# Making the low part of every fourth gate and up chunk by an adding transfer instead of VectorE

## The chip, the cores and the metric

The kernel runs on one core of one Trainium2 chip. The metric is the device time of one execution in microseconds (us). Three runs of the kernel before took 1509.71 to 1509.88 us, median 1509.78 us.

## The reference, cut to what matters

A decoder layer on 256 tokens of width 2048: a normalised projection, two kinds of attention, gates and an output projection, then the part that the change touches, a feed-forward network, and after it a gated embedding and a last norm. All in float32:

```
h = rmsnorm(x, g_ffn)                                    # 256 x 2048
x = x + (silu(h @ w_ffn_gate) * (h @ w_ffn_up)) @ w_ffn_down   # D_FF = 5632
```

w_ffn_gate and w_ffn_up are 2048 x 5632, w_ffn_down is 5632 x 2048.

## The kernel before, in words

Each product is made in three passes of a reduced float32 type (fp32r): a number is split into a high part (rounded to fp32r) and a low part (the number minus its high part), and TensorE adds high x high, low x high and high x low.

**Chunks and units.** Weights stream from HBM in chunks of 512 KB, 128 partitions x 1024 float32. In the feed-forward network a chunk is two row tiles of 512 columns each (KW = 2, WIDE = 512). Four chunks make a unit, and there are four slots (SLOTS), so chunk j of every unit lives in slot j of three buffers: ws (as loaded), hs (high part), ls (low part). One block of 512 feed-forward columns (`ff_pair`) takes four units: two of the gate, two of the up weights. There are 11 blocks (N_FFN), so 44 units and 176 chunks.

**Who does what to a chunk.** SP loads it (L259, `load`) once the low part of the same slot's chunk in the unit before has been made (`slot_free`, semaphore l_split). ScalarE makes the high part (L382, `split_high`) once the chunk has landed and TensorE has finished with the same slot of the unit before (semaphore chunk_used). VectorE makes the low part (L663, `split_low`: ws minus hs) once the high part is there (h_split). TensorE (`by_token`) waits for the high part, does eight matmuls with hs (L1192), waits for the low part (l_split) and does four with ls (L1197); the last counts up chunk_used.

**What lies between the chunks.** After the fourth chunk of a block's first unit TensorE makes eight transposes (L1282, `ff_columns`) of the last block's result, which ScalarE copies (L602, `ff_hi`) and VectorE subtracts (L1014, `ff_low`). After the second unit ScalarE makes the silu (L592), after the fourth VectorE multiplies (L1007).

**Order.** Each engine's instructions stand in a fixed, hand-written order and each engine works through them in that order. GpSimd (POOL) has nothing to do from the end of the attention on. No DMA of the kernel before is issued by GpSimd; SP issues the weights, and ScalarE four small or single transfers.

Of the kernel before, what the change touches and what calls it, by code (L numbers as in the profile page):

```python
# [6 lines left out]
ALU = mybir.AluOpType  # L7
ACT = mybir.ActivationFunctionType
# [17 lines left out]
KW = 2  # L26
# [43 lines left out]
C_PLE = C_DOWN + FF_CH * N_WIDE  # L70
C_END = C_PLE + PLE_CH * N_WIDE
HOOK = 3


D_VB = 1 + 4 + 4 + 4
# [33 lines left out]
def hybrid_layer(nc, c_rows, x, p, positions, g_mix, w_in, b_f, w_o_a, w_o_b, w_out, g_ffn, w_ffn_gate,  # L109
# [125 lines left out]
    sq_sum, rms_sqrt, rms_ready = S("sq_sum"), S("rms_sqrt"), S("rms_ready")  # L235
    p_t, p_high, p_ready = S("p_t"), S("p_high"), S("p_ready")
    ff_silu, ff_s, ff_t, ff_high, ff_ready = map(S, ("ff_silu", "ff_s", "ff_t", "ff_high", "ff_ready"))
    last_used, ple_sig, ple_out, y_scaled = S("last_used"), S("ple_sig"), S("ple_out"), S("y_scaled")
    y_ready_0, y_ready_1 = S("y_ready_0"), S("y_ready_1")

# [3 lines left out]
    @block.sync  # L244
    def _(sp):

        for b in range(2):
            sp.dma_start(x_tok[:, b, :], x_rows[:, b, :]).then_inc(x_loaded[b], 16)
        for n, g in enumerate((g_mix[0], g_ffn[0], g_ple[0])):
            sp.dma_start(gain_rows[n * KT:(n + 1) * KT, :], g.rearrange("(t q) -> t q", q=P)).then_inc(gains_loaded, 16)  # L250
        sp.dma_start(bias_f[F_ROWS, :], b_f[0].rearrange("(h o) -> h o", o=1)).then_inc(bias_loaded, 16)

        def slot_free(u, j):

            sp.wait_ge(l_split, 4 * (u - 1) + j + 1)

        def load(j, src, n=CHUNK):
            parts = src.shape[1]
            sp.dma_start(ws[:, j, 0:n].rearrange("p (t n) -> p t n", t=parts), src).then_inc(w_loaded[j], 16)  # L259


        sp.wait_ge(ring_zero, SLOTS)
        for j in range(SLOTS):
            slot = ws[:, j, 0:SMALL].rearrange("p (t n) -> p t n", t=KC)
            rows = win_t[:, KC * j:KC * j + KC, :]
            for at, col, n in ((0, AT_KI, D_IDX + H_IDX), (F_ROW, AT_FB, HB)):
                sp.dma_start(slot[:, :, at:at + n], rows[:, :, col:col + n]).then_inc(w_loaded[j], 16)

        def columns(u0, units, w, col0):

            with sp.Fori(0, units) as i:
                for j in range(SLOTS):
                    slot_free(u0 + i, j)
                    load(j, w[:, KC * j:KC * j + KC, ds(col0 + i * GROUP, GROUP)])

        columns(U_QI, 4, win_t, AT_QI)
        columns(U_QB, 8, win_t, AT_QB)

        def wide_columns(u0, units, w, col0):

            with sp.Fori(0, units) as i:
                for c in range(K_CH):
                    slot_free(u0 + c // SLOTS + i * (K_CH // SLOTS), c % SLOTS)
                    load(c % SLOTS, w[:, KW * c:KW * (c + 1), ds(col0 + i * WIDE, WIDE)])

        wide_columns(U_VB, 2, win_t, AT_VB)
        wide_columns(U_GA, N_WIDE, win_t, AT_GA)
        columns(U_QA, 6, win_t, AT_QA)
        wide_columns(U_GB, N_WIDE, win_t, AT_GB)
        with sp.Fori(0, N_WIDE) as i:  # L290
            for c in range(K_CH):
                slot_free(U_WO + c // SLOTS + i * 2, c % SLOTS)
                w, t = (wob_t, woa_t)[c // SLOTS], KW * (c % SLOTS)
                load(c % SLOTS, w[:, t:t + KW, ds(i * WIDE, WIDE)])

        sp.wait_ge(o_ready, FREE + HEADS)
        sp.dma_start(p_tok[:, :, :], p_rows).then_inc(p_loaded, 16)
        wide_columns(U_OUT, N_WIDE, wout_t, 0)
        with sp.Fori(0, N_FFN) as i:
            for half, w in enumerate((wgate_t, wup_t)):  # L300
                for c in range(K_CH):
                    slot_free(U_FFN + 2 * half + c // SLOTS + i * 4, c % SLOTS)
                    load(c % SLOTS, w[:, KW * c:KW * (c + 1), ds(i * WIDE, WIDE)])
        for n in range(N_WIDE):
            for c in range(FF_CH):
                at = C_DOWN + FF_CH * n + c
                slot_free(at // SLOTS, at % SLOTS)
                load(at % SLOTS, wdown_t[:, KW * c:KW * (c + 1), WIDE * n:WIDE * (n + 1)])
        for n in range(N_WIDE):
            cols = slice(WIDE * n, WIDE * (n + 1))  # L310
            for c in range(PLE_CH):
                at = C_PLE + PLE_CH * n + c
                slot_free(at // SLOTS, at % SLOTS)
                load(at % SLOTS, wpp_t[:, :, cols] if c == 0 else wpg_t[:, KW * (c - 1):KW * c, cols])

        for n in range(4):
            cols = slice(D_MODEL // 4 * n, D_MODEL // 4 * (n + 1))
            for b in range(2):
                sp.wait_ge((y_ready_0, y_ready_1)[b], n + 1)
                sp.dma_start(out_rows[:, b, cols], out_tok[:, b, cols]).then_inc(out_stored, 16)  # L320
        sp.wait_ge(out_stored, 8 * 16)

    @block.gpsimd
    def _(pool):
# [42 lines left out]
        with pool.Fori(0, HA) as h:  # L367
            stage_head(HB + h, h, h // (HA // HA_KV), D_VA + 1)


    @block.scalar
    def _(act):
# [161 lines left out]
        for n in range(N_WIDE):  # L534
# [5 lines left out]
                act.activation(gates[:, gate, :, cols], gates[:, gate, :, cols], ACT.Sigmoid).then_inc(gate_ready, 1)  # L540
            split_chunks(C_WO + 8 * n + 8, 4)

        def squares(stage, n):

            act.wait_ge(x_new, 4 * stage + n + 1)
# [18 lines left out]
        for n in range(N_WIDE):  # L564
# [5 lines left out]
            else:  # L570
                squares(0, n - 1)
                new_high(0, n - 1, (n - 1) % 2)
            split_chunks(C_OUT + 8 * n + 8, 4)

        def ff_pair(i, step, first=False):

            u = U_FFN + 4 * step + i * 8
            c = step + i * 2
            for j in range(SLOTS):
                split_high(u + 1, j)  # L580
            if first:
                squares(0, 3)
                new_high(0, 3, 1)
                root(0)
            else:
                ff_hi(c - 1, (step + 1) % 2)
            for j in range(SLOTS):
                split_high(u + 2, j)
            if first:
                act.wait_ge(rms_ready, 1)  # L590
            for b in range(2):
# [1 line left out]
            ins.then_inc(ff_silu, 1)  # L593
            for j in range(SLOTS):
                split_high(u + 3, j)
            for j in range(SLOTS):
                split_high(u + 4, j)

        def ff_hi(c, pair):

# [1 line left out]
            act.activation(ff[:, ds(c * 4, 4), 0:TOK], four(side[:, 2 * pair:2 * pair + 2, :]), ACT.Copy).then_inc(ff_high, 1)  # L602

        ff_pair(0, 0, first=True)
        with act.Fori(0, (N_FFN - 1) // 2) as i:
            ff_pair(i, 1)
            ff_pair(i, 2)

        for n in range(N_WIDE):
            at = C_DOWN + FF_CH * n  # L610
# [46 lines left out]
    def _(dve):  # L657
# [314 lines left out]
        for n in range(N_WIDE):  # L972
# [5 lines left out]
                                  ALU.subtract).then_inc(p_ready, 1)  # L978
            else:
                new_low(0, n - 1, (n - 1) % 2)  # L980
            split_chunks(C_OUT + 8 * n + 8, 4)
            dve.wait_ge(chunk_used, C_OUT + 8 * n + 8)
            new_x(n, (n + 1) % 2)

        def ff_pair(i, step, first=False):

            u = U_FFN + 4 * step + i * 8
            c = step + i * 2
            for j in range(SLOTS):
                split_low(u + 1, j)  # L990
            if first:
                new_low(0, 3, 1)
# [2 lines left out]
                dve.wait_ge(rms_ready, 1)  # L995
            else:
                ff_low(c - 1, (step + 1) % 2)
            for j in range(SLOTS):
                split_low(u + 2, j)
            for j in range(SLOTS):  # L1000
                split_low(u + 3, j)
            for j in range(SLOTS):
                split_low(u + 4, j)
            dve.wait_ge(ff_silu, c + 1)
            dve.wait_ge(chunk_used, 4 * (u + 4))
# [9 lines left out]
                              ff[:, ds(c * 4, 4), 0:TOK].bitcast(F32), ALU.subtract).then_inc(ff_ready, 1)  # L1015

        ff_pair(0, 0, first=True)
        with dve.Fori(0, (N_FFN - 1) // 2) as i:
            ff_pair(i, 1)
            ff_pair(i, 2)  # L1020

        for n in range(N_WIDE):
            at = C_DOWN + FF_CH * n
# [51 lines left out]
    def _(pe):  # L1075
# [108 lines left out]
                unit(U_QB + n, U_QB + n, hn, (U_QB + e) % 2)  # L1184
                dots(n)

        def by_token(at, slot, tiles, src, banks, first, last, width=WIDE, halves=False):

            def high_part(b):
                for q, k in enumerate(tiles):  # L1190
# [8 lines left out]
                return mm  # L1199

            pe.wait_ge(h_split, at + 1)
            if halves:
                pe.wait_ge(l_split, at + 1)
                for b in range(2):
                    high_part(b)
                    low_part(b).then_inc(last_used, 1)
            else:
                for b in range(2):
                    high_part(b)
                pe.wait_ge(l_split, at + 1)  # L1210
                for b in range(2):
                    mm = low_part(b)
                mm.then_inc(chunk_used, 1)
# [122 lines left out]
        def ff_pair(i, step, first=False, reused=True):  # L1336
# [5 lines left out]
            else:  # L1342
                pe.wait_ge(ff_silu, pair_n)
            for half in range(2):
                if half == 1 and first:
                    pe.wait_ge(x_new, 4)
                elif half == 1:
                    pe.wait_ge(ff_s, pair_n)
                for c in range(K_CH):
                    if first and half == 0:  # L1350
                        pe.wait_ge(xg_ready, KW * (c + 1))
                    by_token(at + K_CH * half + c, c % SLOTS, range(KW * c, KW * (c + 1)), xg, pair_of(acc, 1 - half), c == 0, c == K_CH - 1)
# [15 lines left out]
        for n in range(N_WIDE):  # L1368
            pe.wait_ge((ff_silu, ff_s, x_new, x_new)[n], (N_FFN, N_FFN, 5, 6)[n])
            for c in range(FF_CH):  # L1370
                if n == 0:
                    pe.wait_ge(ff_ready, (KW * c + 1) // 4 + 1)
                at = C_DOWN + FF_CH * n + c
                by_token(at, at % SLOTS, range(KW * c, KW * (c + 1)), ff, pair_of(acc, (n + 1) % 2), c == 0, c == FF_CH - 1)
# [7 lines left out]
        for n in range(N_WIDE):  # L1382
# [6 lines left out]
            for c in range(PLE_CH):  # L1389
                at = C_PLE + PLE_CH * n + c  # L1390
                if c == 0:
                    by_token(at, at % SLOTS, range(KT_PLE), p_cols, pair_of(side, pair), True, True)
                else:
                    if n == 0:
                        pe.wait_ge(xg_ready, KT + KW * c)
                    by_token(at, at % SLOTS, range(KW * (c - 1), KW * c), xg, pair_of(acc, pair), c == 1, c == K_CH,
                             halves=at == C_END - 1)
                if c == HOOK and n == 0:
                    new_columns(1, 3, 0)

# [41 lines left out]
```

## Time and profile before

| | |
|---|---|
| median of three runs | 1509.78 us |
| the profiled execution's own time | 1509.83 us |
| its span, first to last instruction | 1508.0 us |
| granted TensorE clock, mean | 0.997 |
| TensorE matmuls busy | 1480.2 us, 98% |
| VectorE busy | 855.5 us, 57% |
| ScalarE busy | 692.7 us, 46% |
| GpSimd busy | 50.0 us, 3% |
| moved by DMA | 278.87 MB, mean 185 GB/s |

"Busy" counts the time in which an engine has an instruction running. "PE" is TensorE's matmul side, "PEld" its weight loading, which overlaps it; DVE is VectorE, ACT is ScalarE, POOL is GpSimd, SPq is SP's instruction queue. A group of instructions names its line, its output and input tiles, its shape, how many there are, their busy time and the mean of one, and then how long the engine sat idle just before them and what released it.

### The profile page before, as it was taken

The page shows a single profiled execution, that of the slowest core. Times are in us where ns is not written, and L with a number is a line of the kernel's source. Part 1 is how long each engine was busy: PE and PEld are TensorE (multiplying, and loading weights), DVE is VectorE, ACT ScalarE, POOL GpSimd, SP SyncE. Part 2 cuts the span into 40 slices and gives each one's busy share as a digit, 9 for nine tenths or more (in the row PEclk, how much of TensorE's full clock was granted, in tenths as well). Part 3 has the DMA queues.
Part 4 walks back from the last instruction along what each step waited for, and adds up shares of the span by engine and source line. Part 5 has one row for each costly group of instructions (what it writes and reads, how often), then busy time and mean ns, then how long its engine had stood idle before and what let it go on. Part 6 is the DMA issues. An engine that isn't in the chain of part 4 may idle for free.

```text
span 1508.0 us, 19540 instructions
## 1 busy us (share of the span) xinstructions
PE 1480.2 (98%) x7025; PEld 1241.6 (82%) x7025; DVE 855.5 (57%) x987; ACT 692.7 (46%) x847; POOL 50.0 (3%) x80
## 2 busy tenths in 40 slices
PE   5999999999999999999999999999999999999996
PEld 5888888888888888888888888888888888888885
DVE  6966776657655565555445454444545444454654
ACT  5644444544444544545444444444444343443544
POOL 0021001100210000000000000000000000000000
PEclk9999999999999999999999999999999999999998
DMA  6665565566555665566666666566666666666663
GB/s 191 185 194 177 173 194 178 163 185 197 171 168 168 185 199 181 182 193 186 192 184 194 185 192 194 183 192 184 193 184 193 193 185 194 191 186 195 196 212 109
DMA packets 165486, 278.87 MB, mean 185 GB/s; under 512 B 12920, under 2 KB 50224, under 8 KB 164912
## 3 DMA queue, kind: packets, MB, share of 16 engines
q1 hardware_dynamic: 164832, 275.77, 59.6%
q10 hardware_dynamic: 592, 2.24, 0.4%
q8 instruction: 43, 0.70, 0.2%
q14 instruction: 19, 0.16, 0.0%
HBM read 275.87 MB, written 2.11 MB: 184 GB/s over the span
## 4 chain that ended last, share of the span: by engine, by line
PE 96%; DVE 2%; DMA 1%; ACT 0%; issue 0%; ACTq 0%; DVEq 0%
PE acc L1192 51%; PE acc L1197 26%; PE acc L1088 8%; PE acc L1097 4%; PE side L1192 2%; PE side L1197 1%; PE side L1282 1%; DMA rope_c<-in_rope_rows 1%; DVE ls L663 1%; PE side L1227 0%; DVE hn L718 0%; PE side L1233 0%; PE side L1241 0%; PE side L1242 0%; PE side L1240 0%
## 5 line engine op out<-in xcount | busy, mean ns | idle before, releaser
L663 DVE TENSOR_TENSOR ls<-ws,hs 128x1024 fp32r<-128x1024 f32 (+1 forms) x520 | 633.9, 1226 | 585.0 <-ACT hs L382 581.7
L382 ACT ACTIVATE hs<-ws 128x1024 fp32r<-128x1024 f32 (+1 forms) x520 | 548.0, 1057 | 737.8 <-PE acc L1197 611.0
L1192 PE MATMUL acc<-hs,xg 128*128 128x512 f32 x1664 | 412.4, 390 | 0.0
L1192 PEld LDWEIGHTS acc<-hs,xg 128*128 128x128 f32 x1664 | 311.5, 188 | 64.1
L1197 PE MATMUL acc<-ls,xg 128*128 128x512 f32 x832 | 222.6, 389 | 0.0
L1197 PEld LDWEIGHTS acc<-ls,xg 128*128 128x128 f32 x832 | 156.2, 188 | 32.6
L1192 PE MATMUL acc<-hs,ff 128*128 128x512 f32 x704 | 174.3, 390 | 0.0
L1192 PE MATMUL acc<-hs,hn 128*128 128x512 f32 (+1 forms) x704 | 171.9, 387 | 0.0
L1192 PEld LDWEIGHTS acc<-hs,ff 128*128 128x128 f32 x704 | 131.9, 188 | 27.2
L1192 PEld LDWEIGHTS acc<-hs,hn 128*128 128x128 f32 x704 | 127.1, 188 | 24.2
L1088 PE MATMUL acc<-hn,hs 128*128 128x512 f32 x560 | 139.2, 392 | 0.0
L1088 PEld LDWEIGHTS acc<-hn,hs 128*128 128x128 f32 x560 | 101.5, 189 | 18.9
L1197 PE MATMUL acc<-ls,ff 128*128 128x512 f32 x352 | 94.1, 389 | 0.0
L1197 PE MATMUL acc<-ls,hn 128*128 128x512 f32 (+1 forms) x352 | 90.4, 380 | 0.0
L1097 PEld LDWEIGHTS acc<-hn,ls 128*128 128x128 f32 x560 | 74.2, 191 | 4.7 <-DVE ls L663 0.3
L1197 PEld LDWEIGHTS acc<-ls,ff 128*128 128x128 f32 x352 | 66.1, 188 | 13.7
L1097 PE MATMUL acc<-hn,ls 128*128 128x256 f32 x560 | 75.9, 283 | 0.0
L1197 PEld LDWEIGHTS acc<-ls,hn 128*128 128x128 f32 x352 | 64.2, 188 | 13.1
L1192 PE MATMUL acc<-hs,mixed 128*128 128x512 f32 x256 | 63.6, 391 | 0.0
L1192 PEld LDWEIGHTS acc<-hs,mixed 128*128 128x128 f32 x256 | 47.8, 188 | 9.7
L499 ACT ACTIVATE lg<-lg,neg_max 128x128 f32<-128x128 f32 (+1 forms) x32 | 14.3, 448 | 47.0 <-DVE neg_max L878 47.0
L1197 PE MATMUL acc<-ls,mixed 128*128 128x512 f32 x128 | 34.2, 389 | 0.0
(188 smaller groups left out, 812.0 us busy)
## 6 DMA issues: line engine op xcount, KB each, us to landing
ws<-in_w_in SPq DMA_DIRECT2D x152, 512.0 KB, 3.9
ws<-in_w_ffn_gate SPq DMA_DIRECT2D x88, 512.0 KB, 3.5
ws<-in_w_ffn_up SPq DMA_DIRECT2D x88, 512.0 KB, 3.5
ws<-in_w_ffn_down SPq DMA_DIRECT2D x88, 512.0 KB, 3.6
ws<-in_w_out SPq DMA_DIRECT2D x32, 512.0 KB, 3.7
ws<-in_w_ple_gate SPq DMA_DIRECT2D x32, 512.0 KB, 4.3
ws<-in_w_o_b SPq DMA_DIRECT2D x16, 512.0 KB, 4.1
ws<-in_w_o_a SPq DMA_DIRECT2D x16, 512.0 KB, 3.8
```

The costliest lines, as they stand in the source:

```text
L382: act.activation(hs[:, j, 0:n], ws[:, j, 0:n], ACT.Copy).then_inc(h_split, 1)
L499: act.activation(lg[:, cols], lg[:, cols], ACT.Exp, bias=neg_max[:, b:b + 1], accum_out=sums[:, b:b + 1]).then_inc(exp_done, 1)
L663: dve.tensor_tensor(ls[:, j, 0:n], ws[:, j, 0:n], hs[:, j, 0:n].bitcast(F32), ALU.subtract).then_inc(l_split, 1)
L1088: mm = pe.matmul(acc_of(bank + m, 2 * TOK), hs[:, j, at], src[:, k, :], start=first and q == 0, stop=last and q == len(tiles) - 1)
L1097: mm = pe.matmul(acc_of(bank + m, TOK), ls[:, j, at], src[:, k, 0:TOK], start=False, stop=False)
L1192: pe.matmul(banks[b], src[:, k, part * TOK + b * P:part * TOK + (b + 1) * P], hs[:, slot, q * width:(q + 1) * width], start=first and q == ...
L1197: mm = pe.matmul(banks[b], src[:, k, b * P:(b + 1) * P], ls[:, slot, q * width:(q + 1) * width], start=False, stop=last and q == len(tiles ...
L1282: mm = pe.transpose(bank[m // 2][:, m % 2 * TOK + b * P:m % 2 * TOK + (b + 1) * P], rows[:, b, at + m * P:at + (m + 1) * P], ident[:, :])
```

## The change

In the 44 gate and up units the low part of slot 3 (ADDED) is no longer made by VectorE. ScalarE, right after the high part, writes the negated high part into ls (a copy of ws with scale -1, rounded to fp32r), and GpSimd then issues a transfer that reads the same 512 KB of weights from HBM a second time and adds them onto ls in SBUF. TensorE waits for that transfer's semaphore before the low matmuls of this chunk. SP reloads slot 3 of ws once the negated part has been made. The counts of l_split after these units are lower by 44 (N_ADD). The loops of SP, ScalarE and VectorE are partly unrolled for the first and last steps.

```
+ADDED = SLOTS - 1
+U_ADD = U_FFN
+N_ADD = 4 * N_FFN
+def lows(u, j):
+    return 4 * U_ADD + ADDED * (u - U_ADD) + j + 1
...
+        def slot_taken(u, j):                                  # SP, before a load
+            if j == ADDED:
+                sp.wait_ge(neg_high, u - U_ADD)
+            else:
+                sp.wait_ge(l_split, lows(u - 1, j))
...
+        def add_weights(n, w, rows, cols):                     # GpSimd
+            pool.wait_ge(neg_high, n + 1)
+            pool.dma_start(ls[:, ADDED, :].rearrange("p (t n) -> p t n", t=KW), w[:, rows, cols],
+                           accum_op=ALU.add).then_inc(low_added, 16)
+        for i in range(N_FFN):
+            for half, w in enumerate((wgate_t, wup_t)):
+                for q in range(2):
+                    k = KW * (SLOTS * q + ADDED)
+                    add_weights(2 * half + q + i * 4, w, slice(k, k + KW), slice(i * WIDE, i * WIDE + WIDE))
...
+        def negative_high():                                   # ScalarE
+            act.activation(ls[:, ADDED, :], ws[:, ADDED, :], ACT.Copy, scale=-1.0).then_inc(neg_high, 1)
...
             for j in range(SLOTS):                             # ScalarE, ff_pair
                 split_high(u + 1, j)
+            negative_high()
             if first:
                 squares(0, 3)
...
             for j in range(SLOTS):
                 split_high(u + 2, j)
+            negative_high()
             if first:
                 act.wait_ge(rms_ready, 1)
...
-            for j in range(SLOTS):                             # VectorE, ff_pair, four times
+            for j in range(ADDED):
                 split_low(u + 1, j)
...
             pe.wait_ge(h_split, at + 1)                        # TensorE, by_token
+            low = (l_split, at + 1) if low is None else low
...
                 for b in range(2):
                     high_part(b)
-                pe.wait_ge(l_split, at + 1)
+                pe.wait_ge(*low)
...
+                             low=(low_added, 16 * (u + c // SLOTS - U_ADD) + 16) if c % SLOTS == ADDED
+                             else (l_split, lows(u + c // SLOTS, c % SLOTS)))
```

## Rows read from the trace of the kernel before

**Rows 1.** The page: busy us, share and instructions of each engine; then the chain's shares
```profile
PE 1480.2 (98%) x7025; PEld 1241.6 (82%) x7025; DVE 855.5 (57%) x987; ACT 692.7 (46%) x847; POOL 50.0 (3%) x80
...
PE 96%; DVE 2%; DMA 1%; ACT 0%; issue 0%; ACTq 0%; DVEq 0%
```

**Rows 2.** Busy time by stretch, one inside gate and up; last: PEclk, DMA share, GB/s
```profile
0.00:100.00 100.00, 84.74 (x480) 74.42 (x481) 78.88 (x121) 55.83 (x82) 9.07 (x22) 1.00 0.66 193
...
700.00:1100.00 400.00, 400.00 (x1802) 331.93 (x1801) 199.12 (x172) 171.67 (x171) 0.00 (x0) 1.00 0.62 189
```

**Rows 3.** Waits, 655 to 1135 us: who for whom, us in total, times, longest
```profile
ACT hs L382 <- PE acc L1197: 267.6, 169, 1.7
DVE ls L663 <- ACT hs L382: 237.6, 170, 2.3
```

**Rows 4.** Groups by form, whole span
```profile
L663 DVE TENSOR_TENSOR ls<-ws,hs 128x1024 fp32r<-128x1024 f32 x516 | 631.2, 1230 | 585.0 <-ACT hs L382 581.7 <-DVE sel L824 1.4 <-DVE q_idx L785 0.3
L382 ACT ACTIVATE hs<-ws 128x1024 fp32r<-128x1024 f32 x516 | 545.3, 1060 | 737.8 <-PE acc L1197 611.0 <-PE acc L1097 63.8 <-PE acc L1088 25.1
L1197 PE MATMUL acc<-ls,xg 128*128 128x512 f32 x832 | 222.6, 389 | 0.0
...
L1197 PE MATMUL acc<-ls,hn 128*128 128x512 f32 x320 | 85.9, 390 | 0.0
```

**Rows 5.** Timeline inside one block: start us, length us, engine, line, tiles
```profile
887.46 1.06 ACT L382 ACTIVATE hs<-ws 128x1024 fp32r<-128x1024 f32 x1 [1.66 <-PE acc L1197]
890.18 1.06 ACT L382 ACTIVATE hs<-ws 128x1024 fp32r<-128x1024 f32 x1 [1.66 <-PE acc L1197]
...
897.01 0.87 PEld L1197 LDWEIGHTS acc<-ls,xg 128*128 128x128 f32 x4
...
898.35 1.06 ACT L382 ACTIVATE hs<-ws 128x1024 fp32r<-128x1024 f32 x1 [1.67 <-PE acc L1197]
...
899.33 1.03 ACT L602 ACTIVATE ff<-side 128x1024 f32 x1
```

**Rows 6.** Timeline, later in the same block
```profile
908.82 0.87 PEld L1197 LDWEIGHTS acc<-ls,xg 128*128 128x128 f32 x4
...
911.11 1.25 ACT L592 ACTIVATE silu_g<-acc,rms 128x512 f32<-128x512 f32 x2
```

**Rows 7.** Transfers: kind of issue, count, KB each, median us from issue to landing
```profile
ws<-in_w_ffn_gate SPq DMA_DIRECT2D x88, 512.0 KB, 3.5
...
x_tok<-in_x SPq DMA_DIRECT2D x2, 1024.0 KB, 7.7
...
c_keys<-c_rows ACTq DMA_DIRECT2D x1, 1024.0 KB, 6.2
g_out<-in_g_final ACTq DMA_DIRECT2D x1, 1024.0 KB, 8.0
```

**Rows 8.** The tile ws, 700 to 1100 us: landing of its loads
```profile
DMA to landing us min/median/max: 3.3/3.5/4.6
```

**Rows 9.** Timeline at the c_keys transfer, which runs beside weight loads
```profile
181.89 0.36 ACTq L484 DMA_DIRECT2D c_keys<-c_rows  x1
...
185.36 1.06 ACT L382 ACTIVATE hs<-ws 128x1024 fp32r<-128x1024 f32 x1 [2.48 <-DMA ws<-in_w_in]
...
189.22 1.06 ACT L382 ACTIVATE hs<-ws 128x1024 fp32r<-128x1024 f32 x1 [2.80 <-DMA ws<-in_w_in]
```

**Rows 10.** Timeline at the g_out transfer
```profile
1407.60 12.18 SPq L259 DMA_DIRECT2D ws<-in_w_ple_gate  x5
...
1408.81 0.35 ACTq L629 DMA_DIRECT2D g_out<-in_g_final  x1
```

**Rows 11.** GpSimd's nearest instructions, groups by form
```profile
L354 POOL COPY q_st<-q_cols 128x256 f32 x16 | 18.0, 1126 | 87.1 <-DVE k_cols L902 73.8 <-DVE k_cols L671 12.4
...
L350 POOL TENSOR_TENSOR qi_l<-q_idx,qi_h 128x256 fp32r<-128x256 f32 x8 | 12.8, 1596 | 0.6
```

More of the change, by code:

```diff
@@ L237, in hybrid_layer @@
     ff_silu, ff_s, ff_t, ff_high, ff_ready = map(S, ("ff_silu", "ff_s", "ff_t", "ff_high", "ff_ready"))
+    neg_high, low_added = S("neg_high"), S("low_added")
     last_used, ple_sig, ple_out, y_scaled = S("last_used"), S("ple_sig"), S("ple_out"), S("y_scaled")
@@ L253, in slot_free @@
         def slot_free(u, j):
-            sp.wait_ge(l_split, 4 * (u - 1) + j + 1)
+            if isinstance(u, int) and u > U_ADD + N_ADD:
+                sp.wait_ge(l_split, 4 * (u - 1) + j + 1 - N_ADD)
+            else:
+                sp.wait_ge(l_split, 4 * (u - 1) + j + 1)
+        def slot_taken(u, j):
+            if j == ADDED:
+                sp.wait_ge(neg_high, u - U_ADD)
+            else:
+                sp.wait_ge(l_split, lows(u - 1, j))
         def load(j, src, n=CHUNK):
@@ L298, in _ @@
         wide_columns(U_OUT, N_WIDE, wout_t, 0)
-        with sp.Fori(0, N_FFN) as i:
+        for j in range(SLOTS):
+            slot_free(U_FFN, j)
+            load(j, wgate_t[:, KW * j:KW * (j + 1), 0:WIDE])
+        for half, w in enumerate((wgate_t, wup_t)):
+            for c in range(0 if half else SLOTS, K_CH):
+                slot_taken(U_FFN + 2 * half + c // SLOTS, c % SLOTS)
+                load(c % SLOTS, w[:, KW * c:KW * (c + 1), 0:WIDE])
+        with sp.Fori(1, N_FFN) as i:
             for half, w in enumerate((wgate_t, wup_t)):
                 for c in range(K_CH):
-                    slot_free(U_FFN + 2 * half + c // SLOTS + i * 4, c % SLOTS)
+                    slot_taken(U_FFN + 2 * half + c // SLOTS + i * 4, c % SLOTS)
                     load(c % SLOTS, w[:, KW * c:KW * (c + 1), ds(i * WIDE, WIDE)])
@@ L306, in _ @@
                 at = C_DOWN + FF_CH * n + c
-                slot_free(at // SLOTS, at % SLOTS)
+                if at < C_DOWN + SLOTS:
+                    slot_taken(at // SLOTS, at % SLOTS)
+                else:
+                    slot_free(at // SLOTS, at % SLOTS)
                 load(at % SLOTS, wdown_t[:, KW * c:KW * (c + 1), WIDE * n:WIDE * (n + 1)])
@@ L368, in _ @@
             stage_head(HB + h, h, h // (HA // HA_KV), D_VA + 1)
+        def add_weights(n, w, rows, cols):
[3 more added lines that the diff above has]
+        for i in range(N_FFN):
+            for half, w in enumerate((wgate_t, wup_t)):
+                for q in range(2):
+                    k = KW * (SLOTS * q + ADDED)
+                    add_weights(2 * half + q + i * 4, w, slice(k, k + KW), slice(i * WIDE, i * WIDE + WIDE))
     @block.scalar
@@ L573, in _, with ff_pair @@
             split_chunks(C_OUT + 8 * n + 8, 4)
-        def ff_pair(i, step, first=False):
+        negative_high()
+        def ff_pair(i, step, first=False, more=True):
             u = U_FFN + 4 * step + i * 8
@@ L588, in ff_pair @@
                 split_high(u + 2, j)
+            negative_high()
             if first:
@@ L595, in ff_pair @@
                 split_high(u + 3, j)
+            negative_high()
             for j in range(SLOTS):
                 split_high(u + 4, j)
+            if more:
+                negative_high()
         def ff_hi(c, pair):
@@ L604, in _ @@
         ff_pair(0, 0, first=True)
-        with act.Fori(0, (N_FFN - 1) // 2) as i:
+        with act.Fori(0, (N_FFN - 1) // 2 - 1) as i:
             ff_pair(i, 1)
             ff_pair(i, 2)
+        ff_pair((N_FFN - 1) // 2 - 1, 1)
+        ff_pair((N_FFN - 1) // 2 - 1, 2, more=False)
         for n in range(N_WIDE):
@@ L980, in _, with ff_pair @@
                 new_low(0, n - 1, (n - 1) % 2)
-            split_chunks(C_OUT + 8 * n + 8, 4)
+            split_chunks(C_OUT + 8 * n + 8, 4 if n < N_WIDE - 1 else ADDED)
             dve.wait_ge(chunk_used, C_OUT + 8 * n + 8)
             new_x(n, (n + 1) % 2)
-        def ff_pair(i, step, first=False):
+        def ff_pair(i, step, first=False, more=True):
             u = U_FFN + 4 * step + i * 8
             c = step + i * 2
-            for j in range(SLOTS):
+            for j in range(ADDED):
                 split_low(u + 1, j)
@@ L997, in ff_pair @@
                 ff_low(c - 1, (step + 1) % 2)
-            for j in range(SLOTS):
+            for j in range(ADDED):
                 split_low(u + 2, j)
-            for j in range(SLOTS):
+            for j in range(ADDED):
                 split_low(u + 3, j)
-            for j in range(SLOTS):
+            for j in range(ADDED if more else SLOTS):
                 split_low(u + 4, j)
@@ L1017, in _ @@
         ff_pair(0, 0, first=True)
-        with dve.Fori(0, (N_FFN - 1) // 2) as i:
+        with dve.Fori(0, (N_FFN - 1) // 2 - 1) as i:
             ff_pair(i, 1)
             ff_pair(i, 2)
+        ff_pair((N_FFN - 1) // 2 - 1, 1)
+        ff_pair((N_FFN - 1) // 2 - 1, 2, more=False)
         for n in range(N_WIDE):
@@ L1185, in _, with by_token @@
                 dots(n)
-        def by_token(at, slot, tiles, src, banks, first, last, width=WIDE, halves=False):
+        def by_token(at, slot, tiles, src, banks, first, last, width=WIDE, halves=False, low=None):
             def high_part(b):
@@ L1209, in by_token @@
                     high_part(b)
-                pe.wait_ge(l_split, at + 1)
+                pe.wait_ge(*low)
                 for b in range(2):
@@ L1344, in ff_pair @@
             for half in range(2):
+                u = U_FFN + 4 * step + 2 * half + i * 8
                 if half == 1 and first:
@@ L1351, in ff_pair @@
                         pe.wait_ge(xg_ready, KW * (c + 1))
-                    by_token(at + K_CH * half + c, c % SLOTS, range(KW * c, KW * (c + 1)), xg, pair_of(acc, 1 - half), c == 0, c == K_CH - 1)
+                    by_token(at + K_CH * half + c, c % SLOTS, range(KW * c, KW * (c + 1)), xg, pair_of(acc, 1 - half), c == 0, c == K_CH - 1,
+                             low=(low_added, 16 * (u + c // SLOTS - U_ADD) + 16) if c % SLOTS == ADDED
+                             else (l_split, lows(u + c // SLOTS, c % SLOTS)))
                     if c == HOOK and half == 0:
@@ L1373, in _ @@
                 at = C_DOWN + FF_CH * n + c
-                by_token(at, at % SLOTS, range(KW * c, KW * (c + 1)), ff, pair_of(acc, (n + 1) % 2), c == 0, c == FF_CH - 1)
+                by_token(at, at % SLOTS, range(KW * c, KW * (c + 1)), ff, pair_of(acc, (n + 1) % 2), c == 0, c == FF_CH - 1,
+                         low=(l_split, at + 1 - N_ADD))
                 if c == HOOK and n == 0:
@@ L1391, in _ @@
                 if c == 0:
-                    by_token(at, at % SLOTS, range(KT_PLE), p_cols, pair_of(side, pair), True, True)
+                    by_token(at, at % SLOTS, range(KT_PLE), p_cols, pair_of(side, pair), True, True, low=(l_split, at + 1 - N_ADD))
                 else:
@@ L1396, in _ @@
                     by_token(at, at % SLOTS, range(KW * (c - 1), KW * c), xg, pair_of(acc, pair), c == 1, c == K_CH,
-                             halves=at == C_END - 1)
+                             halves=at == C_END - 1, low=(l_split, at + 1 - N_ADD))
                 if c == HOOK and n == 0:
```

## The prediction

> **What bounds the kernel now.** I read the page first. TensorE's matmuls are busy for 98% of the span and hold 96% of the chain that ended last; VectorE, from which the change takes work, is busy for 57% and holds 2% of the chain [rows 1]. The next view is the table by stretches: inside the gate and up stage TensorE is busy for all 400 of 400 us, VectorE for 199, ScalarE for 172, GpSimd for none, and the DMA engines for 0.62 of the time [rows 2]. The list of waits says why the two helpers idle: ScalarE waited 267.6 us of that stage for TensorE to release slots, and VectorE 237.6 us for ScalarE's high parts; nobody on TensorE's side waited for either [rows 3]. So VectorE is not late, it is fed late, and nothing in this stage is gained by sparing it. The timeline gives the beat: ScalarE's high parts start at 887.46 and 890.18, so a chunk takes 2.72 us on TensorE, which is its twelve matmuls without a gap; from slot 3 of one unit (887.46) to slot 3 of the next (898.35) it is 10.89 us, four chunks [rows 5].
>
> **What is removed.** VectorE loses 44 of its low parts at 1.23 us each, 54 us [rows 4]. They lie under TensorE's matmuls and end nothing: credit 0. If VectorE's load slowed TensorE in some hidden way there would be a gain; the low matmuls are 389 and 390 ns in the stages with xg and with hn, although VectorE's load differs between them [rows 4], so I take 0 here too.
>
> **What is added to ScalarE.** 44 negated copies of the size of a high part, 1.06 us each [rows 4], 47 us in a stage where ScalarE is busy for 172 of 400 us [rows 2]. Back to back a second instruction starts 0.98 us after a high part (898.35 to 899.33), so the negated copy ends 0.98 + 1.06 = 2.04 us after the high part of slot 3 began, inside the 2.72 us until the next slot is released [rows 5]. What stands behind it moves by about 1 us: the copy L602, which nobody needs for blocks, and the silu of 1.25 us [rows 5, 6], whose output is needed at the next block, about eight chunks later. After the silu the next high part starts about 1 us late, with three chunks (8.16 us) until its use. Cost 0; the cover is that lead of three chunks.
>
> **What is moved in SP.** Slot 3 of ws is reloaded after the negated copy instead of after VectorE's low part: 2.04 us against 1.06 + 1.23 = 2.29 us after the high part starts [rows 4]. Nothing is behind it that this hurts: 0.
>
> **What is added to GpSimd and to the DMA engines, and the new wait.** This is the whole question. GpSimd has nothing else to do in this stage [rows 2], so each transfer is issued as soon as the negated copy ends, at 887.46 + 2.04 = 889.50. Before, TensorE began the low part of the same slot (its weight loading) at 897.01 [rows 5]. So the transfer has 7.51 us from issue to landing. In one unit of four the eight transposes stand in this stretch: 898.35 + 2.04 = 900.39 to 908.82, 8.43 us [rows 5, 6]. If it takes L, TensorE stops for L - 7.5 in 33 units and L - 8.4 in 11. Behind the waiting matmuls stands everything of TensorE, in order: the end of this chunk, with it the release of slot 3 to ScalarE, so the next negated copy and the next transfer start late by the same amount. A late transfer is thus paid in every unit and never caught up, while an early one costs nothing at all.
>
> How long is L? The trace before has no adding transfer and none issued by GpSimd. Lower end: a plain 512 KB load issued by SP beside its kind lands in 3.5 us, 4.6 at most [rows 7, 8]. But the adding transfer must read the weights and also the old content of ls, so it handles 1024 KB of input for 512 KB of output. The rows with 1024 KB took 6.2 us (c_keys), 7.7 (x_tok, two at a time at the start) and 8.0 us (g_out); the first and the last ran beside weight loads, as this one would [rows 7, 9, 10]. That such a transfer and the weight loads share the engines is seen at c_keys: ScalarE had to wait 2.48 and 2.80 us for its weights, which it otherwise does not [rows 9]. Upper end: 8.0 us, and the time in which GpSimd writes out the transfer. For that there is no row; its nearest instructions take 1.13 and 1.60 us [rows 11], so 9.6 us in all. I take the row that is nearest in size and company, 8.0, and half of GpSimd's 1.13 us, since a transfer can start before its last piece is written out: L = 8.6 us.
>
> The sum: 33 x (8.6 - 7.5) = 36 us, and 11 x (8.6 - 8.4) = 2 us, together 38 us. The profiled execution took 1509.83 us (span 1508.0 and 1.8 around it), 0.05 us over the median of the three runs, so one number serves: 1510 + 38 = 1548 us. The ends: L at 7.5 or less gives 1510; L = 9.6 gives 33 x 2.1 + 11 x 1.2 = 82 us, 1592. TensorE's clock stays out of the sum: in the first 100 us the matmuls were busy for only 84.74 and 1.00 was granted [rows 2], and a stop of 1.1 in 12 us is less than that.
>
> A rule speaks against this L. The Trainium skill, "DMA: Bandwidth & Descriptors", section "Anatomy of one DMA — SWDGE (gpsimd) path", puts a transfer at about 2.0 us plus its bytes over 436 GB/s; an estimate by it is 3.2 us for 512 KB and 4.4 us for twice the bytes, and the sum would be 0. For 512 KB the trace is near it (3.5), for 1024 KB it is not (6.2 to 8.0) [rows 7], and I go by the rows. For the doubling of the input the same skill has a page, "Collectives: The Full Stack", section "The bandwidth ceiling: the fold count and why AG ≠ RS ≠ AR": an add in the transfer needs two source reads for each piece and ran at about half the rate of a copy; no row of this trace has such an add.
>
> **Rivals.**
>
> (a) *The transfer is hidden anyway*, the other side of my forecast: it lands within 7.5 us, the low part of slot 3 is there before TensorE asks, and the time stays 1510 us, within 1 us. For it: the plain load's 3.5 us leaves 4 us for everything that is special here, c_keys at 6.2 us would still fit with 1.1 us to spare for GpSimd, and g_out and x_tok may be slow for reasons of their own (a row spread over all partitions; two at once at the start). The rule above is of this kind. Against it: the two larger rows. It decides at L = 7.5 us, a point 1.1 us from my value.
>
> (b) *The DMA engines become the bound.* They are busy for 0.62 of a unit's 10.89 us, 6.75 us, so 1.69 us for each of four loads [rows 2, 5]. An adding transfer that costs them twice a load makes 6.75 + 3.4 = 10.1 us, which just fits; from 2.45 loads on it does not. At four loads it is 13.5 us a unit, 2.6 over, and 44 x 2.6 = 115 us: 1625 us. For it: an add may handle its pieces one by one, read and then write. Against it: nothing in the trace shows one. Then weight loads would land late as well, and ScalarE would wait for ws, not only TensorE for the added part.
>
> (c) *Sparing VectorE gives something back*, through a memory port or otherwise, so that TensorE's 2.72 us a chunk shrinks. At 1% of the stage it would be 44 x 0.11 = 5 us: 1505 us. Against it: no matmul that waits, and the same mean at different VectorE loads [rows 3, 4].
>
> That a quarter of the low parts would not leave VectorE is excluded by the code; its count must fall by 44.
>
> **How the numbers follow.** Chances: my forecast (late by 0.1 to 2.4 us a unit) 0.46, hidden (a) 0.40, DMA engines bound (b) 0.11, gain (c) 0.03. The forecast's own range is 1513 to 1600: its upper end is a little past L = 9.6, where the starts of the next transfers crowd. Below 0.2% (3 us) I count as no change, about the least that a measurement of this kernel can tell apart. So faster 0.03, same 0.40, slower 0.46 + 0.11 = 0.57. The range is 1508 to 1600: it holds (a), all of the forecast, and leaves out (c) and most of (b), about 0.13.
>
> **What would show each step.** VectorE's ls group x472 instead of x516 and 54 us less; a new ScalarE group on ls from ws, x44 at 1.06 us, each beginning 0.98 us after a high part of slot 3. GpSimd's transfers with their time to landing: that median is L, and the table of transfers shows it directly; above 7.5 the matmuls of L1197 wait for it, 33 times longer by 0.9 than the other 11. Weight loads landing later than 3.5 us but ScalarE not waiting for ws. A DMA share near 0.85 in the stage instead of 0.62. The down stage unchanged. I am wrong if the median is under 7.5 us (then (a)), if ScalarE waits for ws again and again (then (b)), or if the beat of a chunk that waits for nothing differs from 2.72 us.

## The result and the profile after

The changed kernel takes 1535.45 us (median of four, 1535.25 to 1539.03) against 1509.76 us: ratio 1.0176, 95% interval 1.0163 to 1.0188, 25.7 us slower. The forecast was 1548 us. The profiled execution is the slowest of the four, 1539.03 us with a span of 1537.2, so its own difference to the one before is 29.2 us.

The page's busy line after, and the shares of the chain that ended last (before: [rows 1]):

```profile
PE 1489.0 (97%) x7025; PEld 1238.6 (81%) x7025; DVE 802.7 (52%) x943; ACT 732.8 (48%) x891; POOL 102.4 (7%) x124
...
PE 77%; DMA 15%; issue 3%; ACT 3%; DVE 2%; ACTq 0%; POOL 0%; DVEq 0%; POOLq 0%
```

TensorE has the same 7025 matmuls. What is new is the 15% of DMA and 3% of ScalarE in the chain, which was 96% TensorE. The groups, by form, of the lines that changed (VectorE's low parts: [rows 4]):

```profile
L713 DVE TENSOR_TENSOR ls<-ws,hs 128x1024 fp32r<-128x1024 f32 x472 | 577.1, 1230 | 603.1 <-ACT hs L421 600.0 <-DVE sel L874 1.4 <-DVE q_idx L835 0.3
...
L583 ACT ACTIVATE ls<-ws 128x1024 fp32r<-128x1024 f32 x44 | 45.9, 1042 | 0.0
...
L401 POOL DMA_DIRECT2D ls<-in_w_ffn_gate x22 | 26.4, 1198 | 417.1 <-ACT ls L583 417.1
L401 POOL DMA_DIRECT2D ls<-in_w_ffn_up x22 | 26.2, 1192 | 232.2 <-ACT ls L583 232.2
```

VectorE's low parts are 44 fewer and take 54.1 us less, and it idles 18 us longer for ScalarE instead. GpSimd's instruction for a transfer takes 1.19 us. The queues with their shares of the engines' span, and the transfers with the median from issue to landing ([rows 7]):

```profile
q1 hardware_dynamic: 164832, 275.77, 57.7%
q0 software_dynamic: 11968, 23.07, 9.4%
...
ws<-in_w_ffn_gate SPq DMA_DIRECT2D x88, 512.0 KB, 4.7
ws<-in_w_ffn_up SPq DMA_DIRECT2D x88, 512.0 KB, 4.6
...
ls<-in_w_ffn_gate POOLq DMA_DIRECT2D x22, 512.0 KB, 8.0
ls<-in_w_ffn_up POOLq DMA_DIRECT2D x22, 512.0 KB, 8.1
```

The adding transfers land after 8.0 us, counted from the start of GpSimd's instruction; the weight loads, 3.5 us before, take 4.7. The waits of the stage (655 to 1170 us) that belong to it:

```profile
POOL ls L401 <- ACT ls L583: 639.0, 43, 194.7
...
PEld acc L1249 <- DMA ls<-in_w_ffn_up: 18.7, 19, 2.1
...
PEld acc L1249 <- DMA ls<-in_w_ffn_gate: 12.5, 10, 2.6
```

TensorE's weight side stands still for 31.2 us in 29 waits on the adding transfers (32.8 us in 31 waits over the whole execution); that covers the 29.2 us by which this execution is longer. ScalarE has no wait for ws among the waits of the stage: weight loads became slower but not late. The stage's busy times, 723 to 1123 us ([rows 2]):

```profile
723.00:1123.00 400.00, 384.60 (x1703) 311.37 (x1701) 146.73 (x127) 194.05 (x197) 40.52 (x34) 1.00 0.83 222
```

The DMA engines are at 0.83 instead of 0.62, TensorE is short of 15.4 of 400 us. The chain through one unit, start and length in us:

```profile
881.72 8.40 DMA ls<-in_w_ffn_up
890.12 0.04 issue
890.17 1.22 PE acc L1249 x4
891.38 0.02 issue
891.40 0.05 ACT hs L421
891.46 0.04 issue
891.50 0.04 ACTq L420
891.54 0.83 issue
892.37 1.05 ACT ls L583
893.42 0.29 issue
893.71 8.39 DMA ls<-in_w_ffn_up
```

This is a loop: landing, the four low matmuls (1.22), release of the slot, high part (0.97, seen as ScalarE and "issue"), negated copy (1.05), GpSimd's start (0.29), and the next transfer. It closes in landing + 3.6 us, here 11.99 us. While that is under the 10.89 us of a unit, TensorE sets the pace; the two meet at a landing of 7.3 us. Where the eight transposes stand a unit takes TensorE about 11.77 us (10.89 and 0.88), and the two meet at 8.2 us. The starts of GpSimd's transfers show both kinds:

```profile
905.69 1.19 POOL L401 DMA_DIRECT2D ls<-in_w_ffn_gate  x1 [10.78 <-ACT ls L583]
917.71 1.20 POOL L401 DMA_DIRECT2D ls<-in_w_ffn_gate  x1 [10.84 <-ACT ls L583]
929.49 1.19 POOL L401 DMA_DIRECT2D ls<-in_w_ffn_up  x1 [10.58 <-ACT ls L583]
```

The first of these landed after 8.44 us, and the next began 12.02 us after it: stopped. The second landed after 6.64 us in a unit with transposes, and the next began 11.78 us after it: not stopped. All eleven units with transposes took between 11.76 and 11.80 us; the stops are in the other 33.

### The profile page after: what moved, and what is told of

Read it like the earlier page. It is cut to its first block, busy times and chain, and to the rows that moved or that the text cites. A ratio compares the mean times of both kernels' runs of the same rounds, so it can differ in the third digit from the quotient of the medians.

```text
span 1537.2 us, 19573 instructions
## 1 busy us (share of the span) xinstructions
PE 1489.0 (97%) x7025; PEld 1238.6 (81%) x7025; DVE 802.7 (52%) x943; ACT 732.8 (48%) x891; POOL 102.4 (7%) x124
## 4 chain that ended last, share of the span: by engine, by line
PE 77%; DMA 15%; issue 3%; ACT 3%; DVE 2%; ACTq 0%; POOL 0%; DVEq 0%; POOLq 0%
PE acc L1244 37%; PE acc L1249 21%; DMA ls<-in_w_ffn_up 9%; PE acc L1140 8%; DMA ls<-in_w_ffn_gate 5%; PE acc L1149 4%; PE side L1244 2%; ACT ls L583 2%; PE side L1249 1%; PE side L1335 1%; DMA rope_c<-in_rope_rows 1%; ACT hs L421 1%; DVE ls L713 0%; PE side L1280 0%; DVE hn L768 0%
## 5 line engine op out<-in xcount | busy, mean ns | idle before, releaser
L713 DVE TENSOR_TENSOR ls<-ws,hs 128x1024 fp32r<-128x1024 f32 (+1 forms) x476 | 579.8, 1226 | 603.1 <-ACT hs L421 600.0
L1249 PE MATMUL acc<-ls,xg 128*128 128x512 f32 x832 | 226.6, 394 | 19.8 <-DMA ls<-in_w_ffn_up 11.6
L401 POOL DMA_DIRECT2D ls<-in_w_ffn_gate x22 | 26.4, 1198 | 417.1 <-ACT ls L583 417.1
L583 ACT ACTIVATE ls<-ws 128x1024 fp32r<-128x1024 f32 x44 | 45.9, 1042 | 0.0
```

The source lines that it names most:

```text
L401: pool.dma_start(ls[:, ADDED, :].rearrange("p (t n) -> p t n", t=KW), w[:, rows, cols], accum_op=ALU.add).then_inc(low_added, 16)
L583: act.activation(ls[:, ADDED, :], ws[:, ADDED, :], ACT.Copy, scale=-1.0).then_inc(neg_high, 1)
L713: dve.tensor_tensor(ls[:, j, 0:n], ws[:, j, 0:n], hs[:, j, 0:n].bitcast(F32), ALU.subtract).then_inc(l_split, 1)
L1249: mm = pe.matmul(banks[b], src[:, k, b * P:(b + 1) * P], ls[:, slot, q * width:(q + 1) * width], start=False, stop=last and q == len(tiles ...
```

## The experiments

The theory was that each unit is stopped by landing minus room and that nothing else in the change costs. Rival 1: the second read of the weights costs by itself. Rival 2: any transfer of GpSimd's is that slow, adding or not.

**scratch_add**: the added work without the wait. ScalarE writes the spare buffer again only after the last transfer into it has landed; TensorE waits for none.

```
 # kernel before, and in 40 units:
+act.activation(ls_b[:, :], hs[:, 3, :].bitcast(F32), ACT.Copy, scale=-1.0).then_inc(neg_high, 1)
+pool.dma_start(ls_b..., w[:, k:k + KW, cols], accum_op=ALU.add).then_inc(low_added, 16)   # nobody reads ls_b
```

> The kernel before, with VectorE making all low parts as it did, and beside it in 40 of the 44 gate and up units the negated copy by ScalarE and the adding transfer by GpSimd, into a spare 4 KB per partition that nobody reads; TensorE waits for neither. Theory (only the wait for the landing costs; 8.3 us from the end of the negated copy against 7.5 us of room): 1510 us within 1, while the transfers land as late as in the changed kernel, about 8 us, and the weight loads in 4.5 to 5 us. Rival 1 (the second read of the weights costs by itself, by slowing weight loads or TensorE): at least 1520 us, with ScalarE waiting for ws.

1510.07 us (1509.77 to 1510.33), ratio 1.0002, interval 0.9992 to 1.0011. The busy times of scratch_add, 723 to 1123 us (columns as in [rows 2]), and the landing of its adding transfers:

```profile
723.00:1123.00 400.00, 400.00 (x1802) 331.95 (x1801) 199.10 (x172) 210.66 (x208) 43.05 (x36) 1.00 0.86 237
...
DMA to landing us min/median/max: 6.2/7.7/8.8
```

TensorE is busy for all 400 us with the DMA engines at 0.86 and transfers that land after 7.7 us. Rival 1 is out: traffic, ScalarE's 40 copies and GpSimd's instructions cost nothing by themselves here, and only the wait costs.

**plain_in_place**: the wait without the adding.

```
-pool.dma_start(ls..., w[:, rows, cols], accum_op=ALU.add).then_inc(low_added, 16)
+pool.dma_start(ls..., w[:, rows, cols]).then_inc(low_added, 16)
```

> The changed kernel with the accumulate taken off GpSimd's 44 transfers: same bytes from HBM, same place, same semaphore, same wait, but ls then holds the plain weights, so the low part of these chunks is left out. Theory (the landing is long because the add reads two inputs, so it costs the DMA engines as much as two loads): landing about 5.5 us, inside the 7.5, time 1510 us within 1. Rival 2 (any transfer that GpSimd issues beside this load lands at about 8 us, because of its descriptor writing and of sharing the engines): landing 7.5 us or more and over 1520 us.

1511.31 us (1510.11 to 1512.13), ratio 1.0010 (1.0000 to 1.0019). Its transfers and its queue of GpSimd's:

```profile
q0 software_dynamic: 11968, 23.07, 4.7%
...
ls<-in_w_ffn_gate POOLq DMA_DIRECT2D x22, 512.0 KB, 5.2
ls<-in_w_ffn_up POOLq DMA_DIRECT2D x22, 512.0 KB, 5.2
```

Same count of packets and same bytes as the adding transfers, half the share of engine time (4.7 against 9.4%), and a landing of 5.2 us. Rival 2 is out. Of the 4.5 us by which an adding transfer is later than a plain load of SP's before (8.0 against 3.5), 1.7 come with GpSimd as the issuer and company, and 2.8 with the adding. The median is 1.5 us over before, 0.3 us more than expected; in the profiled execution (span 0.9 us over before's) TensorE waited once, for 0.7 us, for a transfer that landed late, 7.8 us at most against the median of 5.2.

**negate_first**: a little more room.

```
 # ScalarE, unit u:
-high(0), high(1), high(2), high(3), negated(3)
+high(0), high(1), high(2), negated(3), high(3)
 # SP, before it reloads slot 3:
 sp.wait_ge(neg_high, u - U_ADD)
+sp.wait_ge(h_split, 4 * u)
```

> The changed kernel with ScalarE writing the negated copy of slot 3 before its high part instead of after it (SP then waits for both before it reloads the slot), so that each adding transfer starts about 1 us earlier. Theory: room grows from 7.5 to 8.5 us against 8.3 us at the median, so most of the stops go; only the transfers that land later than the median still stop TensorE: 1511 to 1516 us. Rival 1 (traffic costs by itself): about as slow as the changed kernel, 1530 to 1536 us.

1519.46 us (1516.98 to 1521.09), 3.5 us over the upper end of what I had expected. The landing of its adding transfers says why:

```profile
DMA to landing us min/median/max: 7.4/7.7/10.3
```

This loop closes in landing + 2.6 us, so a landing of 8.3 us still fits. The median does, the tail up to 10.3 us does not: TensorE's weight side waited 10.6 us in 9 waits. A forecast with the median alone misses what the late ones cost.

**two_buffers**: much more room.

```
 # as negate_first, and
+ls_b = sb("ls_b", 198, [CHUNK], F32R)          # low part of slot 3 in even units
-act.wait_ge(chunk_used, 4 * (u - 1) + ADDED + 1)   # ahead of the negated copy
+pool.wait_ge(low_added, 16 * n)                # GpSimd, ahead of transfer n
```

> As negate_first, and the negated copies of even units go into a second 4 KB buffer, so that ScalarE needs not wait for TensorE's release of slot 3 and the adding transfer starts about 2.7 us earlier still; GpSimd waits for the transfer before. Theory: room about 11 us against 8.3, no stop is left, 1510 us within 1. Rival 1 (traffic costs by itself): over 1520 us.

1509.99 us (1509.85 to 1510.12), ratio 1.0001 (0.9992 to 1.0011), although its transfers land as late as ever, 8.1 us into ls and 7.5 us into ls_b. This kernel does all that the change does, and costs nothing. It gains nothing either: VectorE was not the bound.

**half_add**: half the bytes.

```
+act.activation(ls[:, ADDED, WIDE:CHUNK], ws[:, ADDED, WIDE:CHUNK], ACT.Copy, scale=-1.0).then_inc(neg_high, 1)
+pool.dma_start(ls[:, ADDED, WIDE:CHUNK], w[:, k, cols], accum_op=ALU.add).then_inc(low_added, 16)
 # VectorE: split_low(u, ADDED, WIDE) in place of split_low(u, ADDED)
```

> Only the second half of slot 3 (512 of 1024 columns, 256 KB) gets its low part by the adding transfer, VectorE makes the first half; the rest as in the changed kernel. Theory: the transfer costs the DMA engines half, lands in about 6 us, and starts about 0.5 us earlier since the negated copy is half as long; room 8.0 us, no stop: 1510 us within 1. Rival (the length is mostly fixed, from the adding as such or GpSimd's writing): landing still over 7.5 us and some stops, 1515 us or more.

1509.69 us (1509.61 to 1509.82), ratio 0.9999; landing 5.7 us at the median, 7.1 at most, GpSimd's instruction 0.85 us. As expected: halving the bytes takes 2.3 us off the landing.

**thin_loads**: the adding transfer nearly alone.

```
 # gate and up loads of blocks 2 to 11:
-load(c % SLOTS, w[:, KW * c:KW * (c + 1), ds(i * WIDE, WIDE)])
+sp.dma_start(ws[:, j, 0:16], w[:, KW * c, ds(i * WIDE, 16)]).then_inc(w_loaded[j], 16)
```

> The changed kernel with the weight loads of blocks 2 to 11 of gate and up cut to 16 columns of one row tile, so most of these weights are left out; the adding transfers stay whole and have the DMA engines nearly to themselves. Theory (landing = a fixed part of about 1.8 us, as a plain load shows, + about 3.3 us of engine time for two inputs + about 1 us for GpSimd, and the rest of the 8 us is sharing with weight loads): landing about 6 us, no stops, 1510 us within 2. Rival (the add is slow on its own, sharing has little part): landing 7.5 us or more, and still over 1525 us.

1512.27 us (1511.65 to 1512.84), ratio 1.0017 (1.0007 to 1.0026), 0.3 us past what I had expected. Its transfers at the median, then two late ones from the critical chain, with the loads that SP issued at the time of the second:

```profile
ls<-in_w_ffn_gate POOLq DMA_DIRECT2D x22, 512.0 KB, 6.0
ls<-in_w_ffn_up POOLq DMA_DIRECT2D x22, 512.0 KB, 6.0
...
690.31 7.64 DMA ls<-in_w_ffn_up
...
1145.90 8.41 DMA ls<-in_w_ffn_up
...
1138.10 20.26 SPq L281 DMA_DIRECT2D ws<-in_w_ffn_down  x8
```

Nearly alone, an adding transfer of 512 KB needs 6.0 us; the other 2.0 us of the 8.0 come with the weight loads beside it. Four of the 44 landed later than 6.2 us (6.7 to 8.4), and just these had whole loads beside them: three in the first block, and the very last, beside the first loads of the down weights. TensorE's weight side waited for two of them, 0.5 and 1.3 us, which covers the 1.9 us by which the profiled execution was over before.

**scratch_more**: half as much adding traffic again.

```
 # scratch_add, and after each adding transfer
+pool.wait_ge(more_added, 16 * (n - 1))
+pool.dma_start(ls_c[:, :], w[:, k, cols], accum_op=ALU.add).then_inc(more_added, 16)   # 256 KB
```

> scratch_add with a second adding transfer of 256 KB in each of its 40 units, into another spare buffer, which nobody waits for but GpSimd: half as much again of adding traffic. If engine time is used up as the queues' shares say (6.75 us for four loads, 3.3 for the adding transfer, 1.65 for the small one: 11.7 us of a unit of 10.89), the DMA engines become the bound and weight loads come late: about 1510 + 40 x 0.8 = 1542 us. Rival (the shares overlap: in scratch_add the DMA engines were busy for 0.86 of the stage and not 0.92, so an adding transfer takes 2.6 us of them and the sum is 6.75 + 2.6 + 1.3 = 10.65): just hidden, 1510 to 1514 us, DMA share 0.95 or more.

1509.92 us (1509.73 to 1511.04). My sum of the queues' shares was wrong and the rival of that expectation right:

```profile
723.00:1123.00 400.00, 400.00 (x1802) 331.98 (x1801) 198.96 (x172) 210.65 (x208) 75.86 (x72) 1.00 0.96 260
...
ACT hs L398 <- DMA ws<-in_w_ffn_gate: 2.2, 3, 0.9
```

The engines are busy for 0.96 of the time and move 260 GB/s, and only now does ScalarE wait for weights, three times. So the DMA engines are not the bound, and some of their time is still left. Sharing them costs all the same, but only through the landing: with the 6.0 us of thin_loads nothing would stop.

**room_less, room_same, room_more**: the start of the transfer shifted by a microsecond either way, on one chip.

```
 # room_less: ScalarE
 act.activation(ls[:, ADDED, :], ws[:, ADDED, :], ACT.Copy, scale=-1.0).then_inc(neg_high, 1)
+act.wait_ge(neg_high, 2 * (u - U_ADD) + 1)
+act.activation(ls[:, ADDED, :], ws[:, ADDED, :], ACT.Copy, scale=-1.0).then_inc(neg_high, 1)
 # room_same: the changed kernel; room_more: negate_first
```

> The changed kernel with the negated copy written twice, the second after the first has ended, so that each adding transfer starts about 1.1 us later and its room shrinks from 7.5 to 6.4 us (7.3 where the eight transposes stand). Theory (each unit is stopped by landing + 0.3 us - room): with a landing of 7.7 to 8.0 us as in the two runs of the changed kernel, 33 x 1.6 to 1.9 + 11 x 0.7 to 1.0, together 61 to 74 us: 1571 to 1584 us. Rival (the cost is set by how often the engines are shared, not by the start): within 5 us of the changed kernel.

> The changed kernel unaltered, beside the other two on one chip, since its time was 1535.45 us in one set of runs and 1526.49 in another. Theory: 1509.8 + 33 x (median landing + 0.3 - 7.5) us, so 1526 with a landing of 7.7 and 1536 with 8.0, whichever this chip shows.

> negate_first unaltered, on the same chip: room 8.5 us. Theory: below room_same by 7 to 17 us, and over 1510 us only by the transfers that land later than 8.2 us. If the time of room_same comes out low here, this one should too.

The changed kernel had also been run once more on its own:

> The changed kernel once more, unaltered, beside the others on this chip. Its first four times were 1535.25 to 1535.57 and one of 1539.03. If the stops come from when transfers land among weight loads, times scatter by a few us between executions, 1533 to 1540, where kernels without stops scatter by less than 1.

| kernel | loop closes in | median landing | time, us (range) | over before |
|---|---|---|---|---|
| room_less | landing + 4.7 | 8.1 | 1592.81 (1587.08 to 1594.63) | 83.0 |
| room_same | landing + 3.6 | 8.0 | 1534.26 (1533.65 to 1535.90) | 24.5 |
| after, first set | landing + 3.6 | 8.0, 8.1 | 1535.45 (1535.25 to 1539.03) | 25.7 |
| after_again | landing + 3.6 | 7.7 | 1526.49 (1526.14 to 1530.72) | 16.7 |
| negate_first | landing + 2.6 | 7.8, 7.7 | 1519.46 (1516.98 to 1521.09) | 9.7 |
| room_more | landing + 2.6 | 7.5 | 1512.28 (1510.41 to 1513.89) | 2.5 |

The rival of room_less, a cost that doesn't depend on the start, is out: 1.1 us less of room cost 58.5 us beside room_same, 1.3 us for each of 44 units on average. It is 9 us over the upper end of what I had expected, 1584 us. One part of that is that I had taken a landing of at most 8.0 us: by the same rule the 8.1 us measured gives 33 x 2.0 + 11 x 1.1 = 78 us over before.

Medians leave out the scatter; single landings don't. I took each of the 44 landings, added 3.6 us (2.6 or 4.7 in the other kernels), subtracted 10.89 us (11.77 where transposes stand) and added up what was over zero. The profiled executions beside it:

| kernel | by the single landings, us | profiled execution over before, us |
|---|---|---|
| after | 28.4 | 29.2 |
| after_again | 15.5 | 16.5 |
| room_same | 25.4 | 26.1 |
| negate_first | 8.9 | 9.7 |
| room_more | 2.8 | 3.3 |
| room_less | 78.1 | 83.5 |

The loop accounts for all but 1 us everywhere, and in room_less for all but 5. There the granted clock in the stage was 0.98 instead of 1.00: five times it fell to 0.5 for 3.4 us. An estimate from that, half of each 3.4 us lost, is at most 5 x 1.7 = 8.5 us, enough for the 5 us left; that they come from it is not shown.

The stage of room_less, 723 to 1123 us, then one unit on its critical chain:

```profile
723.00:1123.00 400.00, 359.84 (x1557) 289.23 (x1556) 133.56 (x116) 207.37 (x211) 36.96 (x31) 0.98 0.74 204
```

```profile
892.50 8.06 DMA ls<-in_w_ffn_gate
...
900.61 1.20 PE acc L1251 x4
...
902.80 1.05 ACT ls L583
903.85 0.02 issue
903.87 1.07 ACT ls L585
904.94 0.29 issue
905.23 7.65 DMA ls<-in_w_ffn_up
```

The second copy (L585) stands in the loop with its 1.07 us and is paid in full. More room on the same chip took 22 of the 24.5 us away, more than the 7 to 17 us that I had expected of room_more: TensorE's weight side waited 3 times for a late landing, where negate_first, the same kernel, had waited 9 times. And the change's own time differs between sets by what its landing differs: 0.3 us of landing x 33 units is 10 us, and the sets with 7.7 and 8.0 us are 7.8 to 9.0 us apart, while before moved by less than 0.1 us. My expectation for after_again, 1533 to 1540 us, was wrong for that reason: I had taken the landing as fixed. What makes the landing differ between sets is not shown.

## Why the prediction was right, step by step

- **What bounds the kernel.** Right. VectorE's 54 us went and nothing came back; with the wait made harmless (two_buffers, half_add, scratch_add) the time is before's within 0.3 us. A chunk that waits for nothing still takes 2.72 us.
- **ScalarE's copies, the moved silu and SP's reload: cost 0.** Right: scratch_add carries 40 of the copies and two_buffers all of the change's moves. The negated copy took 1.04 us and began 0.97 us after the high part, against 1.06 and 0.98 forecast.
- **The room of 7.5 us, and 8.4 at the transposes.** Right to about 0.2 us. The loop meets the unit at a landing of 7.3 us, and of 8.2 us at the transposes, the difference being the 0.29 us from the end of ScalarE's copy to GpSimd's start, which I had counted into the landing.
- **L = 8.6 us, the term that was mis-sized.** It measured 8.0 + 0.29 = 8.3 us. The 0.6 us on top for GpSimd's writing was wrong: the 1.19 us of that instruction lie inside the time to landing, and only 0.29 us come before it. With 8.3: 33 x 0.8 = 26 us, and nothing for the 11 units with transposes (8.4); measured 25.7. That these two agree so closely is luck, since the 8.0 us are those of the slowest execution, which was 29.2 us over before.
- **The row for L, in part luck.** That an adding transfer counts as 1024 KB is borne out by the engines' time, twice a plain one's. But c_keys, also 1024 KB and also beside weight loads, had taken 6.2 us and would have meant no stop; nothing in the rows decided between it and g_out's 8.0. g_out is one 8 KB row sent to all partitions and nothing is added in it, so that it took as long as the adding transfer is a coincidence as far as any run shows. What the runs show is 6.0 us nearly alone and 2.0 us of sharing. The reason for the sharing was also read too strongly: ScalarE waited for weights 8 more times in the kernel before, 7 of them before 71 us, where c_keys was not under way. At c_keys three loads did land after 6.7 to 7.2 us instead of 3.4 to 4.0.
- **Rival (a), hidden.** It was 0.7 us of landing away; the plain transfer in its place (5.2 us) is hidden but for one late landing. The rule behind it is the Trainium skill's, "DMA: Bandwidth & Descriptors", section "Anatomy of one DMA — SWDGE (gpsimd) path", 2.0 us plus bytes over 436 GB/s. An estimate by it is 3.2 us for the plain transfer, which took 5.2 us beside weight loads, and 4.4 us for the adding one, which took 6.0 us nearly alone: the measurements decide against it in both forms, though no run has a plain one alone. The Trainium skill's page "Collectives: The Full Stack", section "The bandwidth ceiling: the fold count and why AG ≠ RS ≠ AR", says that an add needs two source reads and runs at about half the rate of a copy. The trace agrees: adding took twice the engine time, 9.4 against 4.7% of the span for the same packets.
- **Rival (b), DMA engines bound.** Did not happen, at 0.83 in the stage (forecast near 0.85), nor with half as much traffic again.
- **Rival (c), a gain.** Did not happen: two_buffers, with all of the change and no stop, is at 1509.99 us.
- **"33 times longer by 0.9 than the other 11".** Right in where: 31 waits in the 33 plain units, none in the 11 with transposes. The size is not as even, up to 2.6 us, because the landing scatters from 6.6 to 9.8 us.
- **TensorE's clock, left out of the sum.** Right in the number, 1.00 in the stage of the changed kernel. The reason does not carry: I judged by a stretch with TensorE busy for 84.74 of 100 us at 1.00, but in room_less it was busy for 359.84 of 400 us and 0.98 was granted.

## What to carry to other kernels

When work moves to a transfer, find the loop that it closes: landing, use, release of the buffer, preparation, issue. It costs nothing while the loop is shorter than the period of the bound engine, and the full excess each time once it isn't; here the next microsecond was worth 58 us over 44 units, and the one before it 22 us. Before trimming bytes, take an edge out of the loop: a second buffer of 4 KB per partition, with the copy moved ahead, made the very same transfers free. Half the bytes did as well (half_add), but left VectorE half of the work. But ask first whether the engine that is relieved was ever waited for: here it was not, and the best version only equals the kernel before.

## What the runs showed of the hardware

- An adding transfer into SBUF costs the DMA engines about twice a plain one: 3.3 us of all sixteen for 512 KB (9.4% of 1537.2 us over 44; 2.9 us in room_more by its 8.5%, 3.4 in thin_loads by its 9.9%) against 1.6 us (4.7% of 1508.9 us). At the median it landed after 6.0 us nearly alone and 7.5 to 8.1 us beside whole weight loads, which moved 189 GB/s in the kernel before.
- GpSimd's instruction for it took 1.19 us, for the plain one 0.72 us, for an adding one of 256 KB 0.85 us.
- The queues' shares can't be added up to a bound: 6.75 + 3.3 + 1.65 = 11.7 us of work by the shares fitted into a unit of 10.89 us at a busy share of 0.96.
- The same kernel's landing time differed between sets of runs (7.7 and 8.0 us), and with it its time by 9 us, though the kernel before agreed with itself within 0.1 us.
- In room_less the granted clock fell to 0.5 (1.2 of 2.4 GHz) five times in the stage, for 3.4 us each, 0.5 to 1.1 us after the matmuls had begun again from a stop of 1.8 to 3.3 us. Other stops as long were not followed by one, and in the changed kernel, whose longest stop of the matmuls was 2.2 us, it did not fall in the stage.
